# Issuing four accumulating DMAs one weight chunk earlier on GpSimd's queue

## The reference

```python
h = rms_norm(x, norm1)
proj = h @ w_in
# differential attention (4 heads) and compressed / selected / windowed attention (8 heads)
x = x + jnp.concatenate([o_diff, o_nsa], axis=-1) @ w_out
h = rms_norm(x, norm2)
x = x + (jax.nn.silu(h @ w_gate) * (h @ w_up)) @ w_down
return rms_norm(x, final_norm)
```

## Time and profile before

| what | value |
|---|---|
| time, median of 3 runs | 663.83 us (662.12 to 664.99) |
| time of the profiled execution | 662.12 us |
| its span in the trace | 660.3 us |
| PE busy | 646.7 us, 98% |
| DVE, ACT, POOL busy | 68%, 53%, 40% |
| granted TensorE clock | 0.998 of full speed |

### The profile page before, as it was taken

One profiled execution on the slowest core, in us unless ns is written; L12 is line 12 of the kernel. 1 busy time (PEld: TensorE's weight loads), 2 busy tenths in 40 slices (PEclk: granted clock), 3 DMA queues, 4 the chain that ended last, 5 costly groups with the idle time before them and its releaser, 6 DMA issues.

```text
span 660.3 us, 11056 instructions
## 1 busy us (share of the span) xinstructions
PE 646.7 (98%) x3915; PEld 569.7 (86%) x3915; DVE 451.1 (68%) x929; ACT 348.5 (53%) x689; POOL 265.0 (40%) x158
## 2 busy tenths in 40 slices
PE   8999999999999999999999999999999999999996
PEld 7988988898899887888877888899999998888884
DVE  5435447555655687634489988469688797788894
ACT  7546446688665378715332362344444446655663
POOL 4766253674242440224466767344444320000222
PEclk9999999999999999999999999999999999999999
DMA  8989959469794993144699999887677858766553
GB/s 243 270 180 255 280 150 246 124 181 372 218 256 117 246 172 65 32 161 117 160 297 293 294 281 284 216 228 222 189 230 216 255 177 268 253 201 197 185 172 127
DMA packets 114774, 139.22 MB, mean 211 GB/s; under 512 B 5044, under 2 KB 74784, under 8 KB 114720
## 3 DMA queue, kind: packets, MB, share of 16 engines
q1 hardware_dynamic: 97880, 107.35, 51.9%
q0 software_dynamic: 14176, 26.64, 22.5%
q10 hardware_dynamic: 2664, 4.53, 2.0%
HBM read 132.19 MB, written 54.81 MB: 283 GB/s over the span
## 4 chain that ended last, share of the span: by engine, by line
PE 82%; issue 8%; POOL 6%; DVE 2%; ACT 1%; DMA 1%; POOLq 0%; SPq 0%; DVEq 0%; ACTq 0%
PE bank L776 8%; PE bank L778 8%; PE bank L777 8%; PE bank L795 7%; PE bank L797 7%; PE bank L796 7%; PE bank L1107 6%; PE bank L1105 6%; PE bank L1106 6%; PE bank L948 6%; POOL w_lo L728 4%; PE bank L924 3%; PE bank L908 2%; PE bank L909 2%; POOL down_sums L746 1%
## 5 line engine op out<-in xcount | busy, mean ns | idle before, releaser
L728 POOL TENSOR_TENSOR w_lo<-raw,w_hi 128x1024 fp32r<-128x1024 f32 (+1 forms) x76 | 191.6, 2525 | 259.4 <-ACT w_hi L1148 258.8
L1148 ACT CAST w_hi<-raw 128x1024 fp32r<-128x1024 f32 (+1 forms) x141 | 144.1, 1028 | 148.3 <-PE bank L1107 32.2
L795 PE MATMUL bank<-xT_hi,w_hi 128*128 128x512 f32 x272 | 109.0, 401 | 1.6 <-POOL w_lo L728 1.4
L797 PE MATMUL bank<-xT_hi,w_lo 128*128 128x512 f32 x272 | 107.0, 393 | 0.0
L796 PE MATMUL bank<-xT_lo,w_hi 128*128 128x512 f32 x272 | 106.7, 392 | 0.0
L1774 DVE TENSOR_TENSOR w_lo<-raw,w_hi 128x1024 fp32r<-128x1024 f32 x66 | 79.4, 1203 | 35.6 <-ACT w_hi L1148 35.2
L1617 DVE CUSTOM_DVE_ANT_0 bank<-bank,bias 128x128 f32<-128x128 f32 (+3 forms) x96 | 47.5, 497 | 75.0 <-PE bank L909 45.6
L795 PEld LDWEIGHTS bank<-xT_hi,w_hi 128*128 128x128 f32 x272 | 51.2, 188 | 12.8 <-POOL w_lo L728 1.7
L797 PEld LDWEIGHTS bank<-xT_hi,w_lo 128*128 128x128 f32 x272 | 51.1, 188 | 11.7
L1229 ACT ACTIVATE E<-bank,nmax 128x128 f32<-128x128 f32 (+3 forms) x80 | 42.4, 530 | 35.3 <-DVE nmax L1617 34.5
L796 PEld LDWEIGHTS bank<-xT_lo,w_hi 128*128 128x128 f32 x272 | 51.3, 188 | 9.7 <-issue 0.2
(11 more groups left out here) (280 smaller groups left out, 1607.8 us busy)
## 6 DMA issues: line engine op xcount, KB each, us to landing
raw<-mixed_sums SPq DMA_DIRECT2D x24, 512.0 KB, 5.0
raw<-in_w_gate_dram SPq DMA_DIRECT2D x22, 512.0 KB, 6.6
raw<-in_w_in_dram SPq DMA_DIRECT2D x20, 512.0 KB, 6.1
down_sums<-in_w_down_dram SPq DMA_DIRECT2D x20, 512.0 KB, 10.2
raw<-down_sums SPq DMA_DIRECT2D x20, 512.0 KB, 4.2
raw<-in_w_up_dram SPq DMA_DIRECT2D x16, 512.0 KB, 5.2
raw<-in_w_down_dram SPq DMA_DIRECT2D x15, 512.0 KB, 3.5
mixed_sums<-in_w_up_dram SPq DMA_DIRECT2D x12, 512.0 KB, 11.5
```

The source lines that it names most:

```text
L728: nc.gpsimd.tensor_tensor(wv_lo(k)[:, 0:n], raw[:, k % RAW_SLOTS, 0:n], wv_hi(k)[:, 0:n].bitcast(F32), ALU.subtract).then_inc(s_split, 1)
L795: nc.tensor.matmul(bank[:, :], hi, xT_hi[:, kt, :], start=kt == 0, stop=False)
L797: return nc.tensor.matmul(bank[:, :], lo, xT_hi[:, kt, :], start=False, stop=kt == KT - 1)
L1148: nc.scalar.copy(wv_hi(k)[:, 0:n], raw[:, k % RAW_SLOTS, 0:n]).then_inc(s_whi, 1)
```

## The change

The table `add_at` has eight entries of 31 for the pieces 16 to 23. Four of them, for the pieces 16 to 19, become 30. Nothing else differs.

```diff
-    add_at = copy_at[0:16] + [31] * 8 + copy_at[24:]
+    add_at = copy_at[0:16] + [30, 30, 30, 30, 31, 31, 31, 31] + copy_at[24:]
```

## The result

| | before | changed |
|---|---|---|
| median | 661.40 us (7 runs, 660.67 to 664.99) | 667.93 us (7 runs, 665.49 to 669.31) |
| profiled execution, its own time | 662.12 us | 663.55 us |
| its span | 660.3 us | 661.7 us |
| granted TensorE clock, mean of the profiled execution | 0.998 | 0.999 |
| granted clock of the changed kernel's other seven executions | | 0.989 five times, 0.995, 0.996 |

The ratio is 1.0084, with a 95% interval of 1.0058 to 1.0110. The kernel before was timed four more times beside the new one, which moved its median from 663.83 to 661.40. The profiled execution of the changed kernel is 4.4 us faster than its own median, and it is the only one of the eight with a clock of 0.999. So there are two losses to find: one in the trace, and one that this trace doesn't have.

A forecast was written before the change was run, and what follows sets the result against it. PE, busy 646.7 us or 98% of the span, was taken as the bound. Load 34, PE's use of chunk 31, split 32 and the key DMAs each added 0, giving 663.8 us for the median, range 661.5 to 666.2.

The forecast's parts named there:

- load 34: SP's load behind split 31 on the queue: starts at about 220.1 instead of 215.46, with 38 us left, costing 0.
- chunk 31's products: PE's first product with chunks 30 and 31 starts at 255.08, 35 us after split 31's new end: cost 0.
- rival 1: Adds 17 and 21 land later, key DMAs come late, PE stalls 3.5 us: 667.3 us, 0.53% slower; 3 in 100.
- Split 33: On POOL, waits for its own high part made by ACT, so starts at 245.09 as before: gain stops there, 0.
- the price of DVE: Slowing of DVE's instructions beside split 31 at 217.7 to 220.0: 0, or 0.01 us in seven instructions.
- The signs that the prediction had named: It fails if PE's head 3 scores move over 1 us from 254.8, or DVE instructions from 217.7 to 220.0 lengthen.
- The key DMAs: On POOL's queue, released by DVE's evacuation at 247.84; they don't move, so PE's head 3 scores don't either: 0.
- Split 31 therefore runs from about 217.7 to 220.0: On POOL, behind the four adds' 4.6 us of issuing: runs then instead of 213.1 to 215.4, ending 4.6 us later.
- Rows of alike DVE instructions show what a running split costs them: DVE timings beside a split against POOL idle: 0.43 and 0.43 us for a subtraction, 1.43 and 1.42 for seven accumulations.
- rival 2: DVE is slowed by split 31 at its new place, at most 2.36 us: 666.2 us, 0.36% slower; 3 in 100.
- No mechanism at this place can give over 0.5%: Even winning all PE idle time from 210 to 255 us, 2.34 us, gives 661.5 us, 0.35% faster.
- the forecast of no change: Whole kernel: median stays at 663.8 us, with 89 in 100; within 0.5% either way, 0.93.

## Why the prediction was wrong

**What held.** The adds moved as forecast (212.91 against 213.1), load 34 too (219.90 against 220.1), and the delays of load 34 and of chunk 31's products cost nothing: with eight adds early split 31 ends at 239.5 and the median is that of before. The first of the later adds started at 220.66, 3 us ahead of the forecast, since the add of piece 16, for which it waits, landed sooner. Add 23 came at 237.40, 1.7 us earlier than before (forecast 2.3), so rival 1, a longer chain of adds, didn't happen. Split 33 is still released by ACT.

**The step that failed.** It is the price of DVE, "So it is 0, or 0.01 in seven instructions", a term that the sum left out. It measured 3.25 us on L1630, 2.7 us on PE behind it, and in most executions a lower clock on top. The signs that the prediction had named came with it: PE's idle time from 210 to 255 us was 45.00 - 40.45 = 4.55 us and not near 2.3, head 3's scores started at 256.89 and not at 254.83, and a DVE instruction beside the split got longer. The key DMAs came late too (250.56), but only because everything behind DVE was late.

**The place of split 31.** The step "Split 31 therefore runs from about 217.7 to 220.0" was right for the end and wrong for the stretch in which DVE was held. The row begins at 215.73. The earlier trace rows had the sign: the row of split 32 begins at 239.85, before the descriptors of add 23 are done (239.13 + 1.14 = 240.27), and is 2.85 us long. I took the length of a split from the rows without a DMA ahead and put it behind the DMA.

**The rows chosen for DVE.** The step "Rows of alike DVE instructions show what a running split costs them" rested on the earlier trace rows, whose forms all have a PSUM bank among their inputs. I named the rule of the Trainium skill that speaks against the change, a DVE instruction with two SBUF inputs against a GpSimd one that reads SBUF, found that those rows went free by it, and left the form with two SBUF inputs at "no row here shows". It stood in the timeline at 216.58, between the split's old place and the one I gave it. With the split's record at 215.73 it is inside. The instruction that I passed over was the one that mattered: I looked for what DVE does from 217.7 to 220.0 and not for each DVE form from SBUF to SBUF near by.

**The price of rival 2.** It had the mechanism and the sign, at 3 in 100, with "its own length, 2.36 us" as the most it could cost. Two terms were too small. The hold was 3.48 - 0.23 = 3.25 us, since it began 1.1 us before the descriptors ahead of the split were done (216.43 against 217.51). And the sum counted PE's gap once. "No mechanism at this place can give over 0.5%" held for gains; for losses it left out that a gap can bring the clock down, which cost another 4.9 us in the one trace that has it. With the clock, rival 2 would have been 663.8 + 2.7 + 4.9 = 671.4 us, and the chance of slower by over 0.5% would have been the chance of the collision. The 4.9 us could not be read from the trace of before, which is at full clock up to 640 us.

**The base.** 2.4 us of the distance are the kernel before itself, whose median was 663.83 from three runs and 661.40 from seven. Against the later one the forecast of no change would have been 661.4, and the error 6.5 us; that the number 663.8 misses by only 4.1 us is luck. The corrected rival 2 would be 661.4 + 2.7 + 4.9 = 669.0 on that base, 1.1 us over the median.

**What stays open.** That DVE's delay raises the share of executions with a lower clock is shown; which gap brings the clock down is not. Behind a gap of 1.91 to 3.04 us it fell in four traces (three adds early, L1630 as TENSOR_SCALAR, the changed kernel again, and the kernel before with the pieces moved), but not in the first trace of the changed kernel, with the same gap to a hundredth of a microsecond, and not directly behind the gap of 2.96 us. In the changed kernel with the pieces moved it fell half a microsecond into a gap. In three traces it fell (also) between 257 and 262 us. The length of one gap doesn't decide it. The kernel before has such executions too, only fewer: beside the changed kernel's second timing, 2 of its 17 had a clock of 0.991 and 0.992, at 667.27 and 665.41 us. No version beats the kernel before: the best of these, with eight adds early, is equal to it.

## What to carry to other kernels

Before an instruction is moved on GpSimd's queue, list DVE's instructions beside its new place form by form, from the start of its row (with a DMA ahead on the queue, that is the issue of the DMA, not the end of its descriptors): a short DVE instruction from SBUF to SBUF can be held until its end. Where PE is 98% busy, price a new gap on it as its length plus a possible stretch at half clock, here 2.6 and 4.9 us. And when a trace and the median disagree, compare the granted clock of the executions before explaining the trace.

## What the runs showed of the hardware

- An 8-element DVE instruction was held for up to 3.25 us by a GpSimd TENSOR_TENSOR, in the forms SCALAR_TENSOR_TENSOR with two SBUF tensors (3.48 us in all) and TENSOR_SCALAR from SBUF to SBUF (3.49), but not as RECIPROCAL (0.20) or TENSOR_REDUCE (0.41).
- The hold was on while GpSimd was still making the descriptors of an accumulating DMA ahead of that instruction (from 216.43 at the latest, descriptors until 217.51, the split's row of 4.14 us against 2.37 alone), though descriptors alone held nobody (0.23 us in the kernel with eight adds early).
- One gap of 3.03 us on PE was followed by 10.3 us at a granted clock of 0.50, in one trace of the changed kernel and not in the other. In a third kernel the clock fell half a microsecond into a gap, 5 us after one of 1.01 us, so the length of the last gap alone doesn't say when it falls.
